# First attention layer of a three-layer block: attention steps placed between the products of the q/k/v projection

## The reference, cut to what matters

```python
def dilated_group(q, k, v, bias_table, window, dilation):
    ...
    logits = jnp.einsum("bnidhc,bnjdhc->bndhij", qb, kk) * (HEAD_DIM ** -0.5) + bias
    logits = jnp.where(mask[None, :, None, None], logits, NEG_INF)
    m = jnp.max(logits, axis=-1, keepdims=True)
    p = jnp.exp(logits - m)
    den = jnp.sum(p, axis=-1)
    o = jnp.einsum("bndhij,bnjdhc->bnidhc", p, vv)
    ...

def dilated_attention(h, w_qkv, w_o, rel_bias):
    qkv = (h @ w_qkv).astype(jnp.float32).reshape(b_, s, 3, N_HEADS, HEAD_DIM)
    ...
    alpha = jax.nn.softmax(jnp.stack(lses, axis=0), axis=0)
    o = jnp.concatenate([outs[g] * alpha[g][..., None] for g in range(N_GROUPS)], axis=2)
    return o.reshape(b_, s, D_ATTN).astype(h.dtype) @ w_o
```

## Time and profile before

| | us |
|---|---|
| median of 3 runs | 1967.52 (1966.52 to 1971.17) |
| the profiled execution, its own time | 1967.67 |
| its span in the trace | 1965.9 |
| PE busy | 1824.2 (93%) |
| VectorE busy | 1101.8 (56%) |
| ScalarE busy | 671.9 (34%) |

### The profile page before, as it was taken

How to read it: one execution, slowest core, us unless ns; L and a number is a source line. 1 busy time by engine, 2 the same in 40 slices (tenths; PEclk the granted TensorE clock), 3 DMA queues, 4 the chain that set the end, 5 groups by cost and what they waited for, 6 DMA issues and landing times.

```text
span 1965.9 us, 20769 instructions
## 1 busy us (share of the span) xinstructions
PE 1824.2 (93%) x7925; PEld 1419.5 (72%) x7925; DVE 1101.8 (56%) x1285; ACT 671.9 (34%) x957; POOL 224.0 (11%) x136
## 2 busy tenths in 40 slices
PE   6968799999999999699999999989898789999996
PEld 5747488888888886478888888856455568888884
DVE  6999655433444434555432444558745787636654
ACT  4124433222232214433221233365453244413431
POOL 2024120000001000020000003481100310000001
PEclk9979799999999997899999999999998899999998
DMA  4211022322332321022322232423121212312321
GB/s 178 78 43 70 1 78 94 122 83 84 106 111 73 115 85 32 1 70 101 114 89 86 95 121 73 138 93 102 38 70 43 86 43 102 123 65 90 110 89 43
DMA packets 29005, 163.98 MB, mean 83 GB/s; under 512 B 4331, under 2 KB 7019, under 8 KB 12556
## 3 DMA queue, kind: packets, MB, share of 16 engines
q1 hardware_dynamic: 24656, 157.58, 22.9%
q10 hardware_dynamic: 4284, 5.53, 0.9%
HBM read 153.39 MB, written 4.46 MB: 80 GB/s over the span
## 4 chain that ended last, share of the span: by engine, by line
PE 77%; DVE 17%; ACT 4%; issue 2%; POOL 1%; DMA 0%; ACTq 0%; DVEq 0%; SPq 0%; POOLq 0%
PE PS L559 23%; PE PS L560 23%; PE PS L561 23%; DVE CV L1555 3%; DVE T_hid L1555 3%; DVE W_lo L1525 2%; DVE R L1510 1%; DVE H_lo L1505 1%; PE PS L695 1%; PE PS L716 1%; ACT W_hi L950 1%; DVE SSUM L1911 1%; DVE X L2022 1%; PE PS L848 1%; PE PS L754 1%
## 5 line engine op out<-in xcount | busy, mean ns | idle before, releaser
L559 PE MATMUL PS<-H_hi,W_hi 128*128 128x512 f32 x1600 | 641.8, 401 | 42.5 <-DVE W_lo L1525 22.2
L560 PE MATMUL PS<-H_lo,W_hi 128*128 128x512 f32 x1600 | 627.9, 392 | 0.0
L561 PE MATMUL PS<-H_hi,W_lo 128*128 128x512 f32 x1600 | 627.9, 392 | 0.0
L950 ACT ACTIVATE W_hi<-W_raw 128x2048 fp32r<-128x2048 f32 (+2 forms) x132 | 266.6, 2020 | 828.4 <-PE PS L561 828.3
L559 PEld LDWEIGHTS PS<-H_hi,W_hi 128*128 128x128 f32 x1600 | 303.4, 190 | 128.9 <-issue 53.6
L1525 DVE TENSOR_TENSOR W_lo<-W_raw,W_hi 128x2048 fp32r<-128x2048 f32 (+2 forms) x132 | 336.1, 2546 | 43.8 <-ACT W_hi L950 43.6
L561 PEld LDWEIGHTS PS<-H_hi,W_lo 128*128 128x128 f32 x1600 | 303.2, 189 | 64.5
L560 PEld LDWEIGHTS PS<-H_lo,W_hi 128*128 128x128 f32 x1600 | 303.8, 190 | 61.0 <-issue 1.9
L559 PE MATMUL PS<-HID_hi,W_hi 128*128 128x512 f32 x640 | 255.3, 399 | 9.9 <-DVE HID_lo L1631 9.9
L1392 POOL TENSOR_TENSOR SSUM<-SSUM,SQ 128x512 f32<-128x512 f32 x52 | 94.3, 1813 | 1444.8 <-ACT SQ L983 1442.1
L560 PE MATMUL PS<-HID_lo,W_hi 128*128 128x512 f32 x640 | 254.8, 398 | 0.0
(11 more groups left out here) (255 smaller groups left out, 1536.8 us busy)
## 6 DMA issues: line engine op xcount, KB each, us to landing
W_raw<-in_inp SPq DMA_DIRECT2D x13, 1024.0 KB, 4.8
W_raw<-in_pw SPq DMA_DIRECT2D x12, 1024.0 KB, 4.7
W_raw<-in_gu0a SPq DMA_DIRECT2D x11, 1024.0 KB, 4.7
W_raw<-in_gu0b SPq DMA_DIRECT2D x11, 1024.0 KB, 4.8
W_raw<-in_gu1a SPq DMA_DIRECT2D x11, 1024.0 KB, 4.8
W_raw<-in_gu1b SPq DMA_DIRECT2D x11, 1024.0 KB, 4.8
W_raw<-in_gu2a SPq DMA_DIRECT2D x11, 1024.0 KB, 4.7
W_raw<-in_gu2b SPq DMA_DIRECT2D x11, 1024.0 KB, 4.8
```

The lines of the kernel that those rows point to most:

```text
L559: nc.tensor.matmul(dst[:], wh, x_hi[:, k, :], start=(k == first), stop=False)
L560: nc.tensor.matmul(dst[:], wh, x_lo[:, k, :], start=False, stop=False)
L561: return nc.tensor.matmul(dst[:], wl, x_hi[:, k, :], start=False, stop=(k == last))
L950: nc.scalar.activation(W_hi[b][:, 0:n], W_raw[b][:, 0:n], ACT.Copy).then_inc(w_hi, 1)
```

## The change

The units of `qkv` come in another order: q0, k0, v0, q1, k1, q2, k2, v1, v2 (kind and head group). Unit 1 uses the banks PS2 and PS3, all others PS0 and PS1; so PS2 to PS7 stay free for attention. Slots are numbered through, unit j has 16j to 16j+15, and `beside_qkv(g)` on PE, ScalarE and VectorE puts a step behind slot g. A job is now two heads (8 jobs instead of 16), whose score matmuls and value matmuls are issued in turn for the partitions 0 to 63 and 64 to 127.

The steps stand at these slots. Scores of jobs 0 to 7: 34, 46, 58, 70, 82, 94, 114, 122. Transposes: 44, 56, 68, 80, 92, 104, 125, 133. Values of jobs 0 to 6: 52, 60, 72, 84, 127, 135, 142. Transposes of v tiles 0 to 4: 42, 50, 122, 130, 138. Row sums: 82, 84, 106, 108, 134, 136. The last v tile, its transposes, the values of job 7 and the six spreads come behind the projection: two spreads ahead of `wo`'s first unit, and one after each of its first four k. On VectorE the W_lo of a unit stands two slots into the unit that runs meanwhile, and the row chain's last part (`row_factors`) stands at slot 139, ahead of the eviction of unit 8's second half. Each three row operations by group (L1760, L1773) become one of 4x1536. The diff, cut to its core (the moved bodies that only change names are left out):

```diff
+QKV_UNITS = [("q", 0), ("k", 0), ("v", 0), ("q", 1), ("k", 1), ("q", 2), ("k", 2), ("v", 1), ("v", 2)]
+QKV_BANKS = [0, 2] + [0] * 7
...
+            def value_transposes(t):
+
+                pe.wait_ge(qkv_made, evicted("v", t))
+                if t in (2, 4):
+                    pe.wait_ge(row_made, t + 2)
+                elif t:
+                    pe.wait_ge(v_tok, t)
...
+                for blk, c, w, keys in blks:
+                    for i in range(2):
+                        lo = HD * i
+                        k = VQK[lo:lo + HD, 12 + t, :]
+                        k = k[:, P * keys[0]:P * (keys[-1] + 1)] if t < 2 else tokens(k, blk)
+                        last = nc.tensor.matmul(S_BANK[i][:, c:c + w], tokens(VQK[lo:lo + HD, 6 + t, :], blk), k,
+                                                start=True, stop=True)
...
+                    for i in range(2):
+                        lo = HD * i
+                        last = nc.tensor.matmul(PV_BANK[lo:lo + HD, blk * P:(blk + 1) * P], VT[:, t, key, lo:lo + HD],
+                                                PT1[PT_TILES[n][i]][:, x * P:(x + 1) * P], start=first, stop=end)
...
+            for j in range(1, L.n):
+                u = L.base + j
+                pe.wait_ge(w_lo, u + 1)
+                if j == 1:
+                    pe.wait_ge(acc_free, u - 1)
+                for half in range(2):
+                    if j >= 2:
+                        pe.wait_ge(qkv_made, (0 if j == 2 else 2 * (j - 1)) + half + 1)
+                    for k in range(L.kt):
+                        last = product(u % 2, L.kt, half, k, H_hi, H_lo, QKV_BANKS[j] + half)
+                        if k == L.kt - 1:
+                            last.then_inc(acc_ready, 1)
+                        beside_qkv(SLOTS * j + 8 * half + k)
+
+            value_transposes(5)
+            spread(0)
+            spread(1)
+            L = layers["wo"]
+            pe.wait_ge(w_lo, L.base + 1)
+            pe.wait_ge(l_made, 16)
+            for k in range(L.kt):
+                if k == 1:
+                    dilated_values(len(JOBS) - 1)
+                pe.wait_ge(o_lo_made, k + 1)
+                for half in range(2):
+                    last = product(L.base % 2, L.kt, half, k, HID_hi, HID_lo)
+                    if k == L.kt - 1:
+                        last.then_inc(acc_ready, 1)
+                if k + 2 < L.kt:
+                    spread(k + 2)
...
+            split_lo(L, At(0))
             rms(MIX1)
-            for j in range(L.n):
-                u = At(L.base + j)
+            taken_qkv(0, 0)
+            taken_qkv(0, 1)
+            for j in range(1, L.n):
                 for half in range(2):
...
+                    for k in range(L.kt):
+                        if SLOTS * j + 8 * half + k > SLOTS + 2:
+                            beside_qkv(SLOTS * j + 8 * half + k)
+                    taken_qkv(j, half)
+            take_pair(4)
             weighted(0)
             for t in range(6):
                 if t < 5:
+                    if t == 4:
+                        take_pair(5)
                     weighted(t + 1)
                 dve.wait_ge(o_hi_made, t + 1)
```

More of the change, by code:

```diff
@@ L669, in _, with evicted @@
             feed_forward(0, FFN0)
-            linear("qkv", ready=after(h_lo_made, H_BASE[MIX1]), norm=MIX1)
-            for t in range(6):
-                pe.wait_ge(qkv_made, t + 1)
-                if t == 0:
-                    pe.wait_ge(std_made, MIX1 + 1)
-                if t >= 4:
-                    pe.wait_ge(v_tok, t - 3)
+            L = layers["qkv"]
+            S_BANK, T_BANK, PV_BANK, ROW_BANK = PS[2:4], PS[4:6], PS[6], PS[7]
+            def evicted(kind, t):
+                return 2 * QKV_UNITS.index((kind, t // 2)) + t % 2 + 1
@@ L745, in _, with dilated_transposes @@
-            rows(2)
-            dilated_values(len(JOBS) - 1)
-            for t in range(6):
+            def dilated_transposes(n):
+                if n == 0:
+                    pe.wait_ge(std_made, MIX1 + 1)
+                for i in range(2):
+                    pe.wait_ge(e_made, 2 * n + i + 1)
+                    if n:
+                        pe.wait_ge(pt_made, 2 * n + i - 1)
+                    for x, (blk, c, key) in enumerate(chunks(n)):
+                        last = nc.tensor.transpose(T_BANK[i][:, x * P:(x + 1) * P], LE[:, 2 * (n % 2) + i, c:c + P], ident)
+                    last.then_inc(pt_ps, 1)
@@ new lines, in rows @@
+            def rows(i):
+                g, kind = i // 2, i % 2
+                if i in (0, 4):
+                    pe.wait_ge(v_tok, 2 + i // 2)
+                    pe.wait_ge(m_made, 8 if i == 0 else 16)
+                else:
+                    pe.wait_ge(row_made, i)
+                if kind:
+                    pe.wait_ge(e_made, (8, 12, 16)[g])
+                for b in range(4):
+                    last = nc.tensor.matmul(ROW_BANK[0:GROUP_HEADS, b * P:(b + 1) * P],
+                                            MD[:, kind, b, 4 * g:4 * g + 4], ident, start=True, stop=True)
+                last.then_inc(st_ps, 1)
@@ L749, in _, with spread @@
+            def spread(t):
                 if t == 0:
                     pe.wait_ge(rowf, 1)
-                    pe.wait_ge(row_made, 6)
+                    pe.wait_ge(pt_made, 16)
                 if t >= 2:
                     pe.wait_ge(o_made, t - 1)
-                nc.tensor.matmul(PS[6 + t % 2][:], sel[t % 2], ROW_w[:, t // 2, :], start=True,
-                                 stop=True).then_inc(f_ps, 1)
-            linear("wo", HID_hi, HID_lo, ready=after(o_lo_made, 0))
+                nc.tensor.matmul(T_BANK[t % 2][:], sel[t % 2], ROW_w[:, t // 2, :], start=True, stop=True).then_inc(f_ps, 1)
@@ new lines, in beside_qkv @@
+            def beside_qkv(g):
+                if g in VALUES_AT:
+                    dilated_values(VALUES_AT.index(g))
+                if g in VT_AT:
+                    value_transposes(VT_AT.index(g))
+                if g in TURN_AT:
+                    dilated_transposes(TURN_AT.index(g))
+                if g in ROWS_AT:
+                    rows(ROWS_AT.index(g))
+                if g in SCORES_AT:
+                    dilated_scores(SCORES_AT.index(g))
+            unit(L, At(0), H_hi, H_lo, after(h_lo_made, H_BASE[MIX1]))
@@ L758, in _ @@
+            steps(pe, L.n, lambda j: None if j.i is None and j.c == 0 else unit(L, j, HID_hi, HID_lo), first=1)
             feed_forward(1, FFN1)
@@ L1175, in _ @@
+            split_hi(act, L, At(0))
+            std(MIX1)
+            load_bias()
+            for j in range(1, L.n):
+                for s in range(SLOTS):
+                    beside_qkv(SLOTS * j + s)
+                if j < L.n - 1:
+                    split_hi(act, L, At(j))
+            take_values(5)
             for t in range(6):
@@ L1779, in _ @@
+            split_lo(L, At(0))
+            rms(MIX1)
+            taken_qkv(0, 0)
+            taken_qkv(0, 1)
+            for j in range(1, L.n):
+                for half in range(2):
+                    for k in range(L.kt):
[3 more added lines that the diff above has]
+            take_pair(4)
             weighted(0)
@@ L2135 @@
     qkv = g["attn_w_qkv"][0]
-    arrays["qkv"] = rows(np.concatenate([qkv[:, 1536:], qkv[:, :1536]], 1))
+    at = {"q": 0, "k": 768, "v": 1536}
+    arrays["qkv"] = rows(np.concatenate([qkv[:, at[kind] + COLS * g:at[kind] + COLS * (g + 1)] for kind, g in QKV_UNITS], 1))
     arrays["wo"] = rows(g["attn_w_o"][0])
```

337 lines of the change are left out of this document (168 added, 169 removed).

## The result

Before 1967.02 us, the changed kernel 1941.1 us, medians of four runs each (1965.67 to 1971.17, and 1939.09 to 1943.4). The ratio is 0.9864, 95% interval 0.9849 to 0.988: 1.4% less, against 1938 forecast. The profiled execution took 1939.09 us with a span of 1937.3, 28.6 less than the profiled one of before.

What follows compares the result with a forecast made beforehand. PE, busy 93% of the span, was taken as the bound: 125.6 + 7.1 + 27.9 = 160.6 us against 190.1, so 29.5 less than 1967.67 gives 1938.2, median 1938 us; range 1927 to 1953.

Steps and rivals of the forecast that it cites:

- the likeliest case: Whole kernel: the forecast's own case, median 1938 us, 1933 to 1943 by itself, chance 0.55.
- The mixed stage: Projection from unit 1 with attention steps between: products 87.5, insertions 36.7, one wait 1.4, together 125.6 us.
- rival 5: Mixed stage: clock stays at half, making the kernel slower than before, 2053 us over the whole stage; chance 0.02.
- rival 4: Scores and values: the two heads do not run side by side, scores +3.8, values +6.7, 1949 us; chance 0.03.
- Helpers in the stage: Mixed stage: PE waits 1.4 us at slot 50 for VectorE's eviction of v's second half, with no other shortfall.
- Rival 1: Mixed stage: helpers are late, PE waiting 14 us instead of 1.4, giving 1950 us; chance 0.17.
- The long wait: End of projection: PE stands 7.1 us because the eviction of unit 8's second half waits behind the row chain.
- To `wo`'s second unit: After the projection's wait: transposes, spreads, job 7's values and `wo`'s first unit, with waits for HID_lo, 27.9 us.
- I take it back from here: `wo`'s first unit: full clock assumed back from 10.5 us after the wait, some four us after its products began.
- rival 3: `wo`'s first unit: clock stays at half to its end, twelve us of work become 20, 1946 us; chance 0.09.
- bounds 34 to 43: Steps put between the projection's products: transposes, values, scores and row sums together 36.7 us, between 34 and 43.
- Rival 2: The end goes well: full clock there, scores and transposes at low bounds, sum falls 7 to 9, 1930 us; chance 0.12.

Runs made afterwards that it cites:

- The last run: The changed kernel with nothing but full-row spreads, the row factors in a zeroed 128-row tile: 1932.09 us, ratio 0.9837.

## Why the prediction came out as it did

The sign, the range and the likeliest case were right. The median lies 3.1 us above the forecast, and that it lies so near is in part luck, since errors of 5.7 and 3.0 us partly cancelled.

- **The mixed stage**, forecast 125.6, was 122.8. The clock was 1.00, so rival 5 was off, and the insertions were somewhat cheaper than priced. Four score pairs cost 1.30 (from 730.31 to 732.07, less 0.46), not 1.53, which puts a further pair near its low bound of 0.22. The smaller steps cost 1.06 and 1.27, not 1.15 and 1.35. Values were 1.23, forecast 1.28. Heads do run side by side, and rival 4 falls with it. But it was priced at 10.5, and undoing it made the stage 5.2 longer: 2.2 in the scores (priced 3.8, some of it in the first group, which gains nothing) and 3.0 in the values (priced 6.7 for 28 pairs at 0.24; the stage has 26, and they gained 0.11 each).
- **Helpers in the stage**: one wait, at the slot forecast, of 0.83 instead of 1.4, and no wait for exponentials. Rival 1 is off; the next layer's 11% of idle time was no guide.
- **The long wait**, forecast 7.1, was 6.85, behind the chain with the reciprocal. The cause stands by the run without it.
- **The clock at the end of the wait** was down, as forecast.
- **To `wo`'s second unit**, forecast 27.9, measured 33.6: this is the term that was mis-sized, by 5.7. The first product came 6.3 us after the transposes (6.2 forecast), and the waits stood where they were put, if 1.1 us shorter (0.41, 1.44, 1.38, 1.38 against 0.5 and three times 1.75). The step that failed was "I take it back from here". The clock did come back, at 796.8, and was lost again at 803.6 for 17 us. That is rival 3 for most of the unit, which I gave 0.09. I argued and priced it from the standing time alone. The last run shows that with the same waits and 128-row spreads it does not happen, and the one with HID_lo first that with the same spreads and 2.1 us of waits it does not either. So between products it took both, waits and four-row spreads; six such spreads in a row did it without a wait among them. I had read those spreads in before as work at a half clock left over from the idle stretch ahead of them, and not asked whether they themselves kept the clock down.

The balance is -2.8, -0.25 and +5.7 on the stretch, 2.6 us above the 160.6; 1.7 more were gained outside it than the forecast had. The profiled execution is the fastest of the four, and the median lies 2.0 above it.

Some sums of the prediction do not come out. The bounds 34 to 43 follow at the top only: 36.7 less 1.4 is 35.3. Rival 2's 7 to 9 has 4.4 and 1.4 to stand on, since the transposes had no lower bound, which gives 1932 and not 1930. And beside the 24 us of small matmuls at half clock that rival 5 cites stand the next 34 us of the same attention at 0.99, which it leaves out. As for when the clock falls behind a stop, it took 4.1 us in the kernel before (814.06 to 818.2), as the prediction has it, and 2.6 in the changed one; the 3.0 us that two of the expectations give for both fit neither.

The Trainium skill, TensorE: Matmul & The Clock Gate, Part 1 (What's actually happening), says that the clock follows how busy TensorE has been of late. As the profile counts busy time, this case does not agree: PE was busy without a gap and lost the full clock in 7.86 us of four-row spreads, and it kept it with 128 rows and 0.4 us of gaps.

## What to carry to other kernels

Small dependent steps belong between the products of a long dense layer, far enough ahead of their use: here they cost 34.5 us and a wait of 6.85 there, and 77 by themselves. Where a chain of helper work ends in front of the product that restarts TensorE, look at what each engine's queue has ahead of the one result that is awaited, and at the clock behind it. Products over four rows are not cheap where the clock is at stake: with zeroed rows up to 128 the same spread took PE no longer, kept the clock here, and cost one pass of 1.34 us on VectorE that nothing waited for.

## What the runs showed of the hardware

- Four-row float32 spreads (4x512, two passes) took 0.99 us at full clock (1.98 / 2) and 1.77 at half (10.60 / 6). With 128 rows at full clock they took 0.95 (3.79 / 4).
- The granted clock fell from 1.00 to 0.50 under these spreads with PE never idle, 3.3 us after the first of them; under 128-row spreads it stayed at 1.00 in the two runs that had them first.
- After PE stopped altogether the clock fell 2.6 us later in the changed kernel, in the run without the reciprocal and in the last run. That is no constant: in the kernel before it took 4.1 us, in the unmixed run 3.8, with one head after the other 4.3. It rose 3.2 us after the first product of `wo` in the changed kernel, 7.8 us after it with HID_lo first, 9.4 with early rows, and ahead of the first product where the spreads had 128 rows.
- Score pairs over two row halves, four in a step, took 1.16 in turn and 1.71 one head after the other. Value pairs over two column halves took 1.09 and 1.58: nearly the same gain for either kind of split.
